# Strassen products over 12 instead of 8 of the 16 contraction chunks, with two of the three input sums sharing one refilled buffer

## The chip, the cores and the metric

The kernel runs on one core of a Trainium2 chip. The metric is the device time of one execution in microseconds (us). Times given as "of the profiled execution" come from one run that the hardware profiler recorded; its span runs from the first to the last instruction.

## What is computed

One inference step of a streaming encoder layer for 592 tokens (16 meta tokens, 512 prompt frames, 64 sample frames), in float32:

```python
z = jnp.einsum('bld,dc->blc', h, w_in)           # 592 x 2048 times 2048 x 6672
fq, fk, fv, fg, ff, sq, sk, sv, sg = jnp.split(z, idx, axis=-1)
fo = fox_prompt(fq, fk, fv, lf) * jax.nn.silu(fg)            # 16 forgetting heads
so = swa_prompt(sq, sk, sv, sinks, rel_bias) * jax.nn.silu(sg)  # 16 sliding-window heads
out = jnp.einsum('blc,cd->bld', jnp.concatenate([fo, so], axis=-1), w_out)
x = layer_norm(ALPHA * h + out, ln_g, ln_b)
```

`lf` is a log-sigmoid of `ff`, and its running sum enters the scores of the forgetting heads. Keys, values and `lf` are returned too.

## The kernel before, in words

A float32 product is made of three matmuls on a high and a low part of each operand (high by high, high by low, low by high); ScalarE writes the high part as a copy in a rounded format, VectorE the low part as a difference.

The projection has 52 tiles of 128 output columns. Tiles 0 and 1 are made in the opening (`opening_products`); the other 50 are taken two at a time, in 25 **duos** `d` = 1 to 25. The contraction is 2048 long, 16 **chunks** of 128. In a duo the 592 tokens are cut in two halves of 296 (`early`, `late`), the two tiles are the other direction, and over the first `2 * CUT` chunks Strassen's scheme is used: seven block products in place of eight, each over `CUT` chunks. Over the rest plain products are made. A duo is 15 **units** on TensorE (`unit`, u = 0 to 14): 0, 1, 2, 3, 6, 7 and 10 are block products of 3 x `CUT` matmuls; 4, 5, 8, 9, 11, 12, 13 and 14 are plain. Here `CUT` is 4, so that each of the 15 units has 12 matmuls. A matmul streams 296 columns, or 280 in the first half of a gate or query tile, where the meta tokens are not needed.

Three block products need sums of blocks of the input: `sum7` in unit 2, `sum6` in unit 1, `sum3` in unit 7. They are made once in the opening (`opening_splits`) and stay in SBUF, each as high and low part. The seven need sums of weights as well, which VectorE makes for every duo (`make_seven`, `make_five`, `make_six`, `make_four`), after which ScalarE and VectorE split them.

What a duo's weights go through: SyncE's queue loads the front part (`FRONT`, the first `2 * CUT` chunks) and the back part of tile f into `w_raw[f]`, in the order front 1 (after `right_low`), front 0 (after `four_made`), back 1, back 0 of the next duo. Splits and sums have fixed steps: `five_part` at u = 1 (ScalarE) and 2 (VectorE), `right_part` 2 and 4, back of tile 1 at 3 and 5, `four_part` 5 and 6, front of the next duo 7 and 8, `make_seven` and `make_five` 9, `make_six` 10, `seven_part` and `six_part` 11 and 12, back of tile 0 at 13 and 14. VectorE also takes TensorE's results out of PSUM (`take_six`, `take_seven`, `take_five`, and `join` at u = 6, 10, 13 and at the end, which sets `corner_summed`, `side_summed`, `top_summed`, `bottom_summed`). Unit 0 of the next duo waits for `top_summed`, unit 10 for `corner_summed` and `four_low`.

The attention of one pair of heads is woven into the same steps. A **stretch** is one or two duos with one pair: Fox stretches have two duos ("vg", the even one, with a value and a gate tile, then "qk"), and Swa stretches mostly one ("gq", a gate and a query tile: duos 18, 19, 20, 23, 24, 25). For each of five token tiles i, TensorE makes scores (`score`), VectorE adds terms and takes the maximum, ScalarE takes the exponential (`probabilities`) and scales the rows (`scale_rows`), TensorE turns them (`turn`), ScalarE copies what was turned (`keep_turned`), and TensorE multiplies by the values (`values`, which waits for `turned_read`). Scores are at steps 3, 6, 9, 12, 15 in stretches of two duos and at 1, 3, 5, 7, 9 in those of one, each turn is four steps later, and values(2) and values(3) of a gq duo are at step 13. Each engine works its own list in order.

The first stretch is duo 1 alone, without attention. After the opening VectorE and ScalarE make the input sums, and then the forget gates: `gate_inputs`, `gate_ones`, `gate_reciprocals` at s = 3, `gate_logs` at 5, `gate_sums` at 7. TensorE turns the sums after step `GATES_TURNED_AT` (9), VectorE copies them (`keep_gates`) at the end of step 10, and `turn_values`, at step `V_FIRST_AT` (13), waits for that copy (`cq_ready`). `bias_table`, some 30 small copies, is at VectorE's step 13.

After duo 25 the last pair's attention runs beside the first column tile of the output product, and then come the other three and the norm; the change leaves their code as it is, but for the order in which mixed rows are loaded.

## Time and profile before

| | us |
|---|---|
| median of 3 runs | 1024.56 (1023.91 to 1025.81) |
| the profiled execution | 1025.96 |
| its span | 1024.1 |
| opening, up to unit 0 of duo 1 | 42.2 |
| duo 1 | 30.9 |
| duos 2 to 25 | 727 |
| output product and norm | 224 |

A row of a timeline is start, duration, engine, line, operation, what it writes and reads, its shape and the count; a bracket gives the engine's idle time before it and what ended it. A matmul's duration runs longer than the distance to the next one, since they are pipelined: the distance of starts is what it costs.

### The profile page before, as it was taken

How to read it: one execution, taken by the hardware profiler on the slowest of the kernel's cores; microseconds unless marked ns; L12 is line 12 of the kernel's file. 1: busy time of each engine (PE TensorE's matmuls, PEld its weight loads, DVE VectorE, ACT ScalarE, POOL GpSimd, SP SyncE). 2: the span in 40 equal slices, each digit the busy share in tenths (PEclk: the TensorE clock that was granted, in tenths of full speed). 3: DMA queues.
4: the chain of work that ended last, by engine and by line, in shares of the span. 5: the costliest groups of instructions: out<-in, count | busy, mean ns of one | idle time of the engine just before them, and what ended most of it. 6: DMA issues, size and time to landing. Idle time of an engine off the chain costs nothing.

```text
span 1024.1 us, 20283 instructions
## 1 busy us (share of the span) xinstructions
PE 1002.4 (98%) x7287; PEld 940.2 (92%) x7287; DVE 717.8 (70%) x1454; ACT 531.6 (52%) x1217; POOL 66.7 (7%) x125
## 2 busy tenths in 40 slices
PE   8989999999999999999999999999999999999996
PEld 7889999999999999999999999999999888888884
DVE  5989676876868687686867787768787654141685
ACT  5537465564646555564565776656677652111400
POOL 1020100100010010001010000000000000000000
PEclk9999999999999999999999999999999999999998
DMA  8233433132343312333322322231226543222423
GB/s 329 72 100 109 140 110 127 58 109 97 109 139 109 125 54 102 107 109 128 120 75 69 102 81 93 102 105 51 88 81 233 189 171 103 83 82 82 165 68 117
DMA packets 36257, 115.05 MB, mean 112 GB/s; under 512 B 9312, under 2 KB 9728, under 8 KB 33584
## 3 DMA queue, kind: packets, MB, share of 16 engines
q1 hardware_dynamic: 24352, 87.26, 24.7%
q0 software_dynamic: 11856, 27.14, 7.9%
q8 instruction: 31, 0.51, 0.2%
q14 instruction: 18, 0.15, 0.0%
HBM read 99.31 MB, written 18.29 MB: 115 GB/s over the span
## 4 chain that ended last, share of the span: by engine, by line
PE 86%; DMA 5%; DVE 5%; issue 2%; ACT 2%; SPq 1%; DVEq 0%; ACTq 0%
PE ps L1627 28%; PE ps L1637 25%; PE ps L1874 20%; PE ps L1839 5%; PE ps L1813 4%; DMA w_raw<-in_w_all 3%; PE ps L1797 2%; PE ps L1796 2%; DMA x_raw<-in_xT 1%; DVE wl L1094 1%; PE ps L1859 1%; DVE tb L1271 1%; SPq L572 0%; ACT pt L939 0%; PE ps L1817 0%
## 5 line engine op out<-in xcount | busy, mean ns | idle before, releaser
L1627 PE MATMUL ps<-xh,wh 128*128 128x296 f32 (+1 forms) x864 | 261.4, 302 | 1.6 <-DVE wl L1357 1.5
L1627 PE MATMUL ps<-xh,wl 128*128 128x296 f32 (+1 forms) x864 | 257.4, 298 | 0.0
L1627 PE MATMUL ps<-xl,wh 128*128 128x296 f32 (+1 forms) x864 | 257.0, 297 | 0.0
L1874 PE MATMUL ps<-wh,mix_parts 128*128 128x512 f32 x576 | 185.2, 391 | 0.0
L1627 PEld LDWEIGHTS ps<-xh,wh 128*128 128x128 f32 x864 | 163.8, 190 | 5.8 <-issue 3.7
L1627 PEld LDWEIGHTS ps<-xl,wh 128*128 128x128 f32 x864 | 164.0, 190 | 0.0
L1627 PEld LDWEIGHTS ps<-xh,wl 128*128 128x128 f32 x864 | 163.4, 189 | 0.0
L1094 DVE TENSOR_TENSOR wl<-w_raw,wh 128x1024 fp32r<-128x1024 f32 (+1 forms) x150 | 142.9, 953 | 20.4 <-ACT wh L825 9.1
L1874 PEld LDWEIGHTS ps<-wh,mix_parts 128*128 128x128 f32 x576 | 108.1, 188 | 23.5 <-DVE rows L1562 0.4
L917 ACT ACTIVATE tb<-tb,small 128x256 f32<-128x256 f32 (+5 forms) x160 | 81.2, 508 | 92.1 <-DVE small L1290 64.2
L1874 PE MATMUL ps<-wl,mix_parts 128*128 128x512 f32 x320 | 124.9, 390 | 0.0
L1637 PE MATMUL ps<-xh,wh 128*128 128x296 f32 x400 | 121.4, 304 | 1.0 <-ACT vT L977 1.0
L1637 PE MATMUL ps<-xl,wh 128*128 128x296 f32 x400 | 119.3, 298 | 0.0
L1637 PE MATMUL ps<-xh,wl 128*128 128x296 f32 x400 | 119.1, 298 | 0.0
L1637 PE MATMUL ps<-sum_high,wh 128*128 128x296 f32 x300 | 92.0, 307 | 0.0
L1637 PE MATMUL ps<-sum_high,wl 128*128 128x296 f32 x300 | 89.7, 299 | 0.0
L1637 PE MATMUL ps<-sum_low,wh 128*128 128x296 f32 x300 | 89.6, 299 | 0.0
L1090 DVE TENSOR_TENSOR wl<-w_raw,wh 128x1024 fp32r<-128x1024 f32 x32 | 38.1, 1222 | 69.1 <-ACT wh L819 69.0
L929 ACT ACTIVATE tb<-tb,small 128x256 f32<-128x256 f32 (+4 forms) x160 | 71.7, 495 | 10.0 <-DVE small L1305 9.8
L1637 PEld LDWEIGHTS ps<-xh,wh 128*128 128x128 f32 x400 | 75.2, 188 | 1.3 <-ACT vT L977 1.2
L1637 PEld LDWEIGHTS ps<-xl,wh 128*128 128x128 f32 x400 | 75.4, 188 | 0.0
L1637 PEld LDWEIGHTS ps<-xh,wl 128*128 128x128 f32 x400 | 75.1, 188 | 0.0
(196 smaller groups left out, 1721.0 us busy)
## 6 DMA issues: line engine op xcount, KB each, us to landing
w_raw<-in_w_all SPq DMA_DIRECT2D x106, 512.0 KB, 4.4
w_raw<-in_w_all SPq DMA_DIRECT2D x14, 1024.0 KB, 4.8
cbc<-c_rows POOLq DMA_DIRECT2D x16, 360.0 KB, 4.1
x_raw<-in_xT SPq DMA_DIRECT2D x7, 592.0 KB, 9.6
rows<-in_x_p POOLq DMA_DIRECT2D x4, 1024.0 KB, 5.2
out_y_p<-rows SPq DMA_DIRECT2D x16, 256.0 KB, 2.6
mix_rows<-mixT POOLq DMA_DIRECT2D x14, 288.0 KB, 2.4
rel_copies<-rel_rows POOLq DMA_DIRECT2D x8, 384.0 KB, 10.7
```

The source lines that it names most:

```text
L917: nc.scalar.activation(t, t, ACT.Exp, bias=nm, accum_out=total[:, i % 3, head:head + 1]).then_inc(exp_done, 1)
L929: nc.scalar.activation(row, row, ACT.Copy, scale=recip[:, i % 3, head:head + 1]).then_inc(scaled, 1)
L1090: nc.vector.tensor_tensor(wl[slot][:, a], w_raw[slot % 2][:, a], wh[slot][:, a].bitcast(F32), ALU.subtract).then_inc(w_low, 1)
L1094: nc.vector.tensor_tensor(low, raw, high.bitcast(F32), ALU.subtract).then_inc(done, 1)
L1271: ins = nc.vector.scalar_tensor_tensor(out=rows_[:, head, a:b], in0=st.score_out(ps, head, piece, b - a), scalar=cqp[:, i, head:head + 1], ...
L1627: ins = nc.tensor.matmul(ps[:, bank, result(tile, h)], a[f][:, w], b[:, ko, first:first + width], start=(ko == n_first and i == 0), stop=( ...
L1637: ins = nc.tensor.matmul(ps[:, bank, 0:HALF], a[:, w], b[:, j, :], start=(start and j == 0 and i == 0), stop=(stop and j == CUT - 1 and i ...
L1796: nc.tensor.matmul(out, queries, k2[:, head, a:b], start=True, stop=False)
L1797: ins = nc.tensor.matmul(out, queries, k_low[:, head, a:b], start=False, stop=True)
L1813: ins = nc.tensor.transpose(st.turn_out(ps, head, j), tb[:, i % SLOTS, head, first:first + P], ident[:])
L1839: ins = nc.tensor.matmul(ps[head_rows(head), bank, at:at + q], v_nat[:, block_, HD * head:HD * head + HD], moving[:, head, 0:q], start=(j ...
L1874: ins = nc.tensor.matmul(ps[:, bank, :], a, b[slot][:, w], start=(ko == 0 and i == 0), stop=(ko == KO - 1 and i == len(products) - 1))
```

## The change

`CUT` becomes 6, so that block products have 18 matmuls, and the plain units cover `REST` = 2 chunks, 6 matmuls each. The order of units, the steps of the splits and of the attention stay.

`sum6` and `sum3` share one buffer, `sum_both` (high and low part, 1776 KB in all). Both are written to DRAM once (`sum_rows`), and each is loaded back in every duo: `sum3` after unit 1 for unit 7, `sum6` after unit 7 for unit 1 of the next duo. `sum3` is first kept in `x_raw` and split in duo 1 (`last_sum`: ScalarE at step 2, VectorE at step 3).

In the first stretch the parameters move: gates turned after step 11, `keep_gates` at the end of step 12, `turn_values` at 14, `gate_reciprocals` from 3 to 5. `bias_table` goes to GpSimd. SyncE's small loads go behind the loads of x, one weight load goes to ScalarE's queue. GpSimd waits for `sum_low` 4 earlier in its list. ScalarE copies the values before it splits the late block of x. The loads of front parts of duo 1 wait for both halves of the opening's weights.

```diff
-CUT = KO // 4
+CUT = 3 * KO // 8
+REST = (KO - 2 * CUT) // 2
-GATES_TURNED_AT, TABLE_AT, V_FIRST_AT = 9, 13, 13
+GATES_TURNED_AT, V_FIRST_AT = 11, 14
-MIX_PARTS = [(0, 2), (2, 5), (5, 8), (8, 12), (12, 14)]
+MIX_PARTS = [(0, 2), (2, 6), (6, 9), (9, 12), (12, 14)]
...
+        sum7_high, sum7_low = (sb(f"sum{n}", [P, CUT, HALF], F32R) for n in ("7_high", "7_low"))
+        sum_both = sb("sum_both", [P, 2, CUT, HALF], F32)
...
         def _(sp):
-            sp.dma_start(wff, w_ff).then_inc(wff_loaded, 16)
...
             for f in range(2):
-                sp.wait_ge(w_low, f + 1)
+                sp.wait_ge(w_low, f + 3)
                 load_part(1, f, FRONT, front_loaded)
             for f in range(2):
-                sp.wait_ge(w_low, f + 3)
                 load_part(1, f, BACK, back_loaded)
+            sp.wait_ge(sum_low, 2)
+            sp.dma_start(sum_rows[0], sum_both[:].rearrange("p a b c -> p (a b c)")).then_inc(sums_stored, 16)
             sp.wait_ge(back_low[0], 1)
             load_part(2, 0, BACK, back_loaded)
+            sp.wait_ge(sum_low, 4)
+            sp.dma_start(sum_rows[1], sum_both[:].rearrange("p a b c -> p (a b c)")).then_inc(sums_stored, 16)
+            sp.wait_ge(sums_stored, 32)
...
+            def load_sums(i, used, loaded):
+
+                sp.wait_ge(unit_done, used)
+                sp.dma_start(sum_both[:].rearrange("p a b c -> p (a b c)"), sum_rows[i]).then_inc(loaded, 16)
+
+            def load_three(d):
+
+                load_sums(1, UNITS * (d - 1) + 2, three_loaded)
+
+            def load_duo(d):
+
                 load_next_front(d, 1)
                 load_next_front(d, 0)
                 load_next_back(d)
+                load_sums(0, UNITS * (d - 1) + 8, six_loaded)
                 sp.wait_ge(back_low[0], d + 1)
                 load_part(d + 2, 0, BACK, back_loaded)
...
-                nc.vector.tensor_tensor(raw3[:], x12, raw6[:], ALU.subtract).then_inc(sum_made, 1)
+                dve.wait_ge(gates_summed, 1)
+                nc.vector.tensor_tensor(x11, x12, raw6[:], ALU.subtract).then_inc(sum_made, 1)
...
+            def last_sum():
+
+                dve.wait_ge(sum_high, 4)
+                low_of(both_low, x_raw[:, first_x, early], both_high, sum_low)
...
                 elif u in (4, 5):
                     if u == 4:
                         pe.wait_ge(back_low[0], d)
-                    ins = plain(0, 0, duo[0], TOP, range((u - 2) * CUT, (u - 1) * CUT), None)
+                    ins = plain(0, 0, duo[0], TOP, rest(u - 4), None)
...
                 elif u == 7:
+                    if st.first:
+                        pe.wait_ge(sum_low, 4)
+                    else:
+                        pe.wait_ge(three_loaded, 16 * d - 16)
```

## Rows read from the trace of the kernel before

**Rows 1.** Part 1 of the page: busy time of each engine.
```profile
PE 1002.4 (98%) x7287; PEld 940.2 (92%) x7287; DVE 717.8 (70%) x1454; ACT 531.6 (52%) x1217; POOL 66.7 (7%) x125
```

**Rows 2.** Windows: length, each engine's busy time (count), TensorE clock, DMA share, GB/s.
```profile
0.00:25.60 25.60, 22.39 (x138) 18.03 (x138) 15.35 (x16) 15.14 (x16) 2.77 (x14) 1.00 0.89 329
42.20:73.10 30.90, 27.45 (x192) 26.97 (x193) 26.87 (x64) 14.96 (x28) 5.67 (x12) 0.94 0.34 110
68.97:72.39 3.42, 3.42 (x16) 3.42 (x15) 2.86 (x13) 1.95 (x3) 0.00 (x0) 0.50 0.00 0
254.34:286.27 31.93, 31.93 (x263) 31.52 (x262) 25.63 (x53) 19.46 (x45) 2.19 (x3) 1.00 0.34 111
286.27:314.01 27.74, 27.74 (x223) 27.12 (x222) 18.76 (x40) 14.05 (x31) 2.69 (x5) 1.00 0.30 101
373.75:407.40 33.65, 32.33 (x263) 31.52 (x262) 25.63 (x53) 19.56 (x45) 2.19 (x3) 1.00 0.31 106
618.44:649.87 31.43, 31.43 (x262) 30.51 (x261) 24.80 (x57) 21.97 (x61) 1.77 (x3) 1.00 0.24 83
```

**Rows 3.** Chain that ended last, in order of time: start, us, what, count.
```profile
134.28 4.89 PE ps L1637 x36
...
384.15 7.59 DMA w_raw<-in_w_all
```

**Rows 4.** Groups by form: count, then busy us and mean ns of one.
```profile
L1094 DVE TENSOR_TENSOR wl<-w_raw,wh 128x1024 fp32r<-128x1024 f32 x75 | 91.5, 1220 | 17.1 <-ACT wh L825 9.1 <-ACT wh L831 7.9
L1094 DVE TENSOR_TENSOR wl<-w_raw,wh 128x512 fp32r<-128x512 f32 x75 | 51.4, 685 | 3.3
L831 ACT ACTIVATE wh<-w_raw 128x1024 fp32r<-128x1024 f32 x50 | 52.4, 1047 | 0.2
L837 ACT ACTIVATE wh<-w_sum 128x512 fp32r<-128x512 f32 x25 | 15.6, 626 | 2.2 <-DVE w_sum L1110 1.8
```

**Rows 5.** Timeline of duo 20 (gq), step 9 to values(2).
```profile
636.99 0.34 PE L1796 MATMUL ps<-k,q 128*128 128x192 f32 x1
...
638.41 0.29 PE L1627 MATMUL ps<-xl,wh 128*128 128x280 f32 x1
638.54 0.29 PE L1627 MATMUL ps<-xh,wl 128*128 128x280 f32 x1
...
639.13 0.69 DVE L1110 TENSOR_TENSOR w_sum<-w_raw 128x512 f32<-128x512 f32 x1
...
642.01 0.63 ACT L837 ACTIVATE wh<-w_sum 128x512 fp32r<-128x512 f32 x1
...
643.77 0.57 ACT L939 ACTIVATE pt<-ps 128x512 f32<-128x512 f32 x1
...
644.48 0.44 PE L1839 MATMUL ps<-pt,v_nat 128*64 128x128 f32 x4
```

**Rows 6.** Timeline of duo 8 (vg) before turn(1).
```profile
270.74 1.04 ACT L825 ACTIVATE wh<-w_raw 128x1024 fp32r<-128x1024 f32 x1
...
272.75 1.11 ACT L929 ACTIVATE tb<-tb,small 128x384 f32<-128x384 f32 x2
...
273.63 0.83 PE L1813 MATMUL ps<-ident,tb 128*128 128x128 f32 x6
```

**Rows 7.** Timeline, end of duo 7 (qk): the join behind `top_summed`, next unit 0.
```profile
251.47 0.46 DVE L1200 TENSOR_TENSOR mid_part<-ps,mid_part 128x296 f32<-128x296 f32 x1
...
254.34 0.30 PE L1637 MATMUL ps<-xh,wh 128*128 128x296 f32 x1
```

**Rows 8.** Timeline of the first stretch: TensorE's first unit, VectorE's copy, `turn_values`.
```profile
42.19 0.41 PE L1637 MATMUL ps<-xh,wh 128*128 128x296 f32 x1 [0.96 <-ACT vT L977]
...
67.33 0.15 DVE L1446 COPY cq<-ps 64x16 f32<-64x16 f32 x1
...
67.64 0.27 PE L1859 MATMUL ps<-ident,v_twice 128*32 128x128 f32 x1 [2.27 <-DVE cq L1446]
```

**Rows 9.** Part 6 of the page: DMA issues, KB each, median us to landing.
```profile
w_raw<-in_w_all SPq DMA_DIRECT2D x14, 1024.0 KB, 4.8
```

More of the change, by code:

```diff
@@ L572, in _ @@
                     sp.dma_start(x_raw[:, x_part(i), :], xT[:, x_part(i), :]).then_inc(x_loaded[i], 16)
-                else:
+                elif i != 1:
                     slot, a = w_part(i)
@@ L576, in _ @@
                 if what == "x" and i == 1:
+                    sp.dma_start(wff, w_ff).then_inc(wff_loaded, 16)
+                if what == "x" and i == X_PARTS - 1:
                     for dst, src in ((gate_half(bf, 0), b_f), (gate_half(bf, 1), b_f), (lfc, lf_cache), (relT, rel),
@@ L680, in _, with bias_table @@
             pool.wait_ge(own_made, 3)
+            def bias_table():
+                pool.wait_ge(small_loaded, 5 * 16)
+                for a, b, bucket in bias_runs():
+                    ins = nc.gpsimd.tensor_copy(bias_rows[:, a:b],
+                                                relT[:, bucket:bucket + 1].broadcast_to([16, b - a]))
+                ins.then_inc(bias_made, 1)
             def first_loads(st):
@@ L1016, in run @@
                             right_part(d, (unit_done, st.after(k, 1)))
+                        if st.first and u == 2:
+                            last_sum(st)
                         if u == 3:
@@ L1495, in run @@
                             five_part(d)
+                        if st.first and u == 3:
+                            last_sum()
                         if u == 4:
@@ L1642, in of_tile, with rest @@
                 return wh[f][:, part], wl[f][:, part]
+            def rest(i):
+                return range(2 * CUT + i * REST, 2 * CUT + (i + 1) * REST)
             def of_x(ko, columns):
@@ L1690, in unit @@
                         pe.wait_ge(back_low[1], d)
-                    ins = plain(1, 0, duo[1], SIDE, range((u - 6) * CUT, (u - 5) * CUT), None)
+                    ins = plain(1, 0, duo[1], SIDE, rest(u - 8), None)
                 elif u == 10:
@@ L1696, in unit @@
                 elif u in (11, 12):
-                    ins = plain(0, 1, duo[0], TOP, range((u - 9) * CUT, (u - 8) * CUT), None)
+                    ins = plain(0, 1, duo[0], TOP, rest(u - 11), None)
                 else:
@@ L1700, in unit @@
                         pe.wait_ge(under_made, d)
-                    ins = plain(1, 1, duo[1], BOTTOM, range((u - 11) * CUT, (u - 10) * CUT), 2 * CUT)
+                    ins = plain(1, 1, duo[1], BOTTOM, rest(u - 13), 2 * CUT)
                 ins.then_inc(unit_done, 1)
```

88 lines of the change are left out of this document (45 added, 43 removed).

## The prediction

> **What bounds the kernel now.** I read the page first: TensorE is busy for 1002.4 us, 98% of the span, with VectorE at 70% and ScalarE at 52% [rows 1]. A busy share alone doesn't say that shorter work on TensorE shortens the kernel, so I read windows next. A vg duo (duo 8), a qk duo and a gq duo have TensorE busy for their whole length, 31.93, 27.74 and 31.43 us [rows 2]: there is no idle time to recover, and every matmul taken away is worth its full pitch, as long as nothing else is just behind it. The same windows say who might be: in the vg and the gq duo VectorE is busy for 25.6 and 24.8 us and ScalarE for 19.5 and 22.0 us. The third reading is therefore the timeline at those places where TensorE takes over from ScalarE or VectorE: how long was the result there before it was used? That slack, not the busy share, decides this change.
>
> **Part 1, the matmuls.** 36 matmuls take 4.89 us, 0.136 us each [rows 3]; of 280 columns one takes 0.13 [rows 5]. Each duo gets 7 x 2 x 3 = 42 more in block products and 8 x 2 x 3 = 48 fewer in plain units. A vg or qk duo loses 36 wide and 12 narrow ones, 6.4 us, and gains 5.7: -0.73. A gq duo loses 24 and 24, 6.3 us: -0.65. With 19 and 6 of them that is 13.9 + 3.9 = -17.8 us.
>
> **Part 2, what VectorE and ScalarE get.** VectorE takes 1.22 us for 1024 elements and 0.685 for 512 [rows 4], so 0.15 + 1.045 per thousand: 0.95 for 768 and 1.75 for 1536. Per duo the front part costs 0.53 more, two back parts 1.07 less, five splits and four sums 9 x 0.27 = 2.4 more: +1.87. ScalarE, by its rows 0.21 + 0.82 per thousand, gets 0.42 - 0.84 + 5 x 0.21 = +0.6. Both have room by the share, 47 us on VectorE's 718. But the work is not spread evenly, and neither is what TensorE loses: steps with a block product get 0.81 us longer, plain ones 0.8 shorter. From unit 7 to unit 0 of the next duo there are six plain units and two block products, so the time is 3.2 us shorter there, just where seven, five, six and the front part are made.
>
> **Part 3, gq duos.** The chain in duo 20 [rows 5]: scores at 636.99, VectorE's `make_seven` at 639.13, `make_five`, the join, ScalarE's copies of q, seven high at 642.01, six high, scaling, `keep_turned` at 643.77 to 644.34, `values` at 644.48. The last row has no idle time ahead of it, so TensorE came there by itself, and the result was there 0.14 before: the slack is about 0.1. After the change, seven and five are 0.27 longer each, ahead of the join, and seven and six high 0.21 each: the chain takes 0.96 longer. TensorE goes through units 9, 11 and 12 at 0.8 less each and unit 10 at 0.8 more: it is there 1.6 us sooner. Stall: 0.96 + 1.6 - 0.1 = 2.4, I take 2.35. It stands in duos 18, 19, 20, 23 and 24: 11.8 us. In 18 and 23 VectorE enters late from the qk duo (below) and the front part reaches ScalarE late, +1 each (bounds 0 and 2). Duo 25 has no seven and six, but the 1.6 us; its slack is larger, +0.7. Sum: +14.5, bounds 8 and 20.
>
> **Part 4, vg duos.** In duo 8 ScalarE's front copy is at 270.74, the first scaled rows of tile 1 are ready at about 273.35, and TensorE turns them at 273.63 [rows 6]: slack 0.3. From scores(0) to this turn TensorE will need 0.7 less (plain units outweigh). VectorE's list in between (right, four +0.54, back -0.54, a wait of 0.4 for the exponential absorbed) is 0.45 shorter, ScalarE's front copy is 0.43 longer: stall 0.45 as the low end. What adds to it is the load of front 0. It is issued after `four_made`, at about 13.3 us in the duo. It is now 768 KB, behind 768 KB for tile 1 and behind `sum3`. For 1776 KB no row exists: 1024 KB take 4.8 us [rows 9] and the opening moves 329 GB/s [rows 2], so 4.8 + 0.77 MB / 0.329 = 7.1 us; bounds 4.8 and 8.3 (in proportion). `sum3` is issued at 5 and lands at 12, four before unit 7 needs it. Front 0 then lands at 18.3 to 20, against 18.4 when ScalarE is free: up to 1.6 more stall. The trace shows such a wait already: a front load of 7.59 us is on the chain [rows 3], and that duo takes 33.65 us against 31.93 [rows 2]; a third of that difference, 0.6, I take as the mean of the eight vg duos, already paid. I take a stall of 1.3 here and 0.2 at the next turn (the effect of part 3, with more slack), less 0.6 already there: +0.9 for each of 8, +7.2, bounds -2 and +14.
>
> **Part 5, qk duos.** The join behind `top_summed` ends at 251.93, unit 0 starts at 254.34: slack 2.4 [rows 7]. TensorE needs 2.1 us less from unit 9 to there, and the chain of six, seven low, six low and ScalarE's seven is 0.8 longer: stall 0.5 in nine qk duos (3 to 17, 22), and 0.3 in duo 21: +4.8, bounds 0 and 8.
>
> **Part 6, the first stretch.** TensorE now waits 2.27 us for VectorE's gate copy, done at 67.5 [rows 8], so VectorE's list sets this time, and all that is put ahead of the copy counts in full. Four sums of x and four low parts grow from 1184 to 1776 elements: 8 x 0.62 = 4.95. The weight work of duo 1 and of the next front, sums included: +3.2. `keep_gates` goes behind seven low and six low: 1.9. The loads of duo 2's front parts are behind the store of `sum3` on SyncE's queue, with a wait for it: `sum3` is split in step 3, at about 56, stored by 63, fronts land at 67 to 69, while VectorE is through with `gate_sums` by 68: it waits some 3 us for ScalarE's front copy. Against that the x loads start about 2 us earlier, for the small loads are behind them: -1.5. The copy is done at 67.5 + 11.5 = 79. `bias_table` on GpSimd takes 2.2 us off VectorE, but behind this wait. TensorE then goes through one unit, not two: duo 2 starts 9.5 us later than now. Before that the wait for `vT` [rows 8] stays about as it is. Beside the -0.73 already counted this is +10.2, bounds 4 and 13.
>
> **One rule beside a row.** After the 2.27 us wait the clock was at 0.50, the lower of its two levels, 1.2 GHz, for 3.42 us [rows 2], and units 13 and 14 cost 0.8 us more each. The Trainium skill (TensorE: Matmul & The Clock Gate, "What's actually happening") says that the throttled state is the default and activity releases it; by that rule, which the trace supports here, new stalls can cost more than their own length. That is a rival below.
>
> **The sum.** -17.8 + 14.5 + 7.2 + 4.8 + 10.2 = +18.9 us. Store and loads of the sums, mixed rows in other portions and the output stage cost nothing by themselves: the loads have four to eight us of slack, and the portions have the last units of duo 25 ahead of them; without that cover the first output step would wait 2 or 3 us. The profiled execution took 1025.96, span 1024.1 plus 1.9 around it, and is 1.4 above the median; the difference goes on the median: 1024.56 + 18.9 = 1043.5, say 1043.
>
> **Rivals.**
> (a) The clock falls in the gq duos too. The wait there is as long as the one after which it fell, and small matmuls follow. At 1.7 us for each of six: 1053. For: the one row. Against: duo 12's stall of 1.5 us left the clock at 1.00.
> (b) Transfers bind. If the big loads get 220 GB/s beside the others (two thirds of the opening's 329), front 0 lands 2 us later again: +2 in eight vg duos, +1.6 in six gq duos, +26: 1069. Against: the DMA share is 0.24 to 0.34 now and gets to about 0.5.
> (c) Faster: slack is larger than I read. If `keep_turned` and `top_summed` stay ahead of TensorE, because the joins start earlier with the shorter units, parts 3 and 5 vanish and part 4 is at its low end: -17.8 - 2 + 10 = 1015. It turns to faster when the stalls of parts 3 to 6 stay below 17.8 together. Against: the slack of 0.1 in rows 5 is read directly.
> (d) The change balances out: low ends of parts 3 and 6, the rest at nothing: within 0.2%.
>
> **Numbers.** Forecast 1043 (1033 to 1051): 0.54. (a) 0.18, (b) 0.11, (c) 0.12, (d) 0.05. Faster 0.13, same 0.05, slower 0.82, where 0.2% (2 us) is about what a measurement can tell from no change. The range leaves out (b)'s upper part and most of (c): 1024 to 1062.
>
> **What would show it.** In the new profile: idle before `values` (ScalarE's `pt` copy as releaser) of some 2.3 us in each gq duo; idle before turn(1) in vg duos, with front loads on the chain; unit 0 behind VectorE's join in vg duos; duo 2 starting near 82 us; no wait on the sums. VectorE busy near 770 us. If gq duos last under 31 us, part 3 is wrong, and if duo 2 starts before 76 us, part 6.

## The result and the profile after

The changed kernel takes 1138.51 us (median, 1132.37 to 1142.33), the kernel before 1025.12 beside it (1023.91 to 1025.81). The ratio is 1.1104, 95% interval 1.1065 to 1.1142. The forecast was 1043, the range 1024 to 1062: the sign was right, the size off by 95 us. The profiled execution took 1138.23, its span is 1136.7 against 1024.1.

The page after: busy time of each engine (as in [rows 1]), the chain that ended last by engine, and the two largest kinds of transfer (KB each, median us from issue to landing).

```profile
PE 1017.3 (89%) x7137; PEld 948.2 (83%) x7137; DVE 764.5 (67%) x1423; ACT 552.2 (49%) x1217; POOL 83.4 (7%) x156
...
PE 52%; DMA 17%; DVE 13%; issue 9%; ACT 8%; DVEq 0%; SPq 0%; ACTq 0%
...
sum_both<-sum_rows SPq DMA_DIRECT2D x48, 1776.0 KB, 7.7
w_raw<-in_w_all SPq DMA_DIRECT2D x52, 768.0 KB, 7.0
```

TensorE's busy time rose by 15 us although it has fewer matmuls, and its share fell from 98% to 89%. The first goes with a lower clock (0.963 over the span, 0.995 before), the second is waiting. So the next view is the list of TensorE's waits: first of the kernel before, then of the changed one. Columns: who waits for whom, us in total, times, longest.

```profile
PE ps L1813 <- ACT tb L929: 3.2, 4, 1.3
PE ps L1859 <- DVE cq L1446: 2.3, 1, 2.3
```
```profile
PE ps L1860 <- ACT tb L963: 41.0, 10, 5.9
PE ps L1676 <- DVE mid_part L1243: 22.7, 9, 4.4
PE ps L1906 <- DVE mixT L1362: 11.2, 7, 2.6
PE ps L1906 <- DVE cq L1486: 11.1, 1, 11.1
PE ps L1886 <- ACT pt L973: 10.9, 7, 1.8
PE ps L1886 <- ACT pt_meta L975: 3.2, 5, 0.9
```

Each line is one place of the schedule: the turns of the vg duos (`tb`), unit 0 behind the join (`mid_part`), `turn_values` of the qk duos (`mixT`) and of the first stretch (`cq`), `values` of the gq duos (`pt`, `pt_meta`). 100 us stand there, and before 5.5 at the first and the fourth place and nothing at the others. All of these places but the third were in the prediction; the first is several times what it said.

Windows of the changed kernel, for [rows 2]: the opening, duo 1, the low clock behind its wait, duo 8 (vg), duo 9 (qk), duo 12 (vg), duo 20 (gq).

```profile
0.00:25.60 25.60, 22.05 (x127) 17.36 (x128) 16.64 (x17) 15.46 (x16) 2.79 (x14) 1.00 0.93 349
45.10:86.34 41.24, 28.13 (x186) 27.40 (x186) 32.98 (x50) 18.33 (x30) 11.45 (x33) 0.83 0.47 171
75.66:89.31 13.65, 5.69 (x25) 5.68 (x26) 10.29 (x24) 7.59 (x17) 2.84 (x7) 0.50 0.28 85
292.49:331.78 39.29, 34.30 (x256) 33.65 (x256) 28.06 (x55) 21.89 (x48) 2.19 (x3) 0.91 0.47 164
331.78:362.41 30.63, 27.28 (x218) 26.24 (x216) 19.90 (x37) 13.29 (x29) 2.71 (x5) 1.00 0.67 235
433.04:473.13 40.09, 34.73 (x255) 34.08 (x256) 27.98 (x55) 21.78 (x48) 2.19 (x3) 0.87 0.44 161
714.91:748.38 33.47, 31.31 (x256) 29.83 (x254) 26.49 (x57) 22.68 (x61) 1.77 (x3) 1.00 0.52 186
```

The vg duo takes 39.29 against 31.93, the qk duo 30.63 against 27.74, the gq duo 33.47 against 31.43; of those shown only the qk and the gq duo keep the clock at 1.00. Summed over the trace, from the start of one duo to the next, the 112.6 us of span stand in: the time up to duo 2 +13.3, the eight vg duos 2 to 16 +50.8, the eight qk duos 3 to 17 +25.7, the six gq duos +18.3, duos 21 and 22 +6.1, the output stage -1.4.

Why a vg duo is 7 us longer is seen in duo 8, in the chain that ended last (start, us, what) and in the timeline beside it, for [rows 6]:

```profile
305.97 9.60 DMA w_raw<-in_w_all
```
```profile
315.67 1.48 ACT L859 ACTIVATE wh<-w_raw 128x1536 fp32r<-128x1536 f32 x1 [4.66 <-DMA w_raw<-in_w_all]
...
318.12 1.10 ACT L963 ACTIVATE tb<-tb,small 128x384 f32<-128x384 f32 x2
...
318.77 1.54 PE L1860 MATMUL ps<-ident,tb 128*128 128x128 f32 x6 [4.99 <-ACT tb L963]
```

Front 0, 768 KB, is 9.6 us on its way and lands at 315.57, 23.1 us into the duo. ScalarE has been idle for 4.66 us by then, and TensorE waits 4.99 at turn(1). The prediction had it land at 18.3 to 20. It isn't the refill ahead of it that is in the way: the 1776 KB for `sum3` were issued at 297.68 and landed 7.4 us later, before front 0 was issued. What else is under way from 297 on is a copy of 384 KB, `rel_copies<-rel_rows`, on GpSimd's queue: issued at 297.01, it lands 17.9 us later. The list of transfers of the kernel before, then of the changed one:

```profile
rel_copies<-rel_rows POOLq DMA_DIRECT2D x8, 384.0 KB, 10.7
```
```profile
rel_copies<-rel_rows POOLq DMA_DIRECT2D x8, 384.0 KB, 18.3
```

### The profile page after: what moved, and what is told of

Its sections match the earlier page's. It is cut to its first block, busy times and chain, and to the rows that moved or that the text cites. A ratio compares the mean times of both kernels' runs of the same rounds, so it can differ in the third digit from the quotient of the medians.

```text
span 1136.7 us, 20065 instructions
## 1 busy us (share of the span) xinstructions
PE 1017.3 (89%) x7137; PEld 948.2 (83%) x7137; DVE 764.5 (67%) x1423; ACT 552.2 (49%) x1217; POOL 83.4 (7%) x156
## 4 chain that ended last, share of the span: by engine, by line
PE 52%; DMA 17%; DVE 13%; issue 9%; ACT 8%; DVEq 0%; SPq 0%; ACTq 0%
PE ps L1676 21%; PE ps L1921 18%; DMA w_raw<-in_w_all 16%; PE ps L1666 6%; DVE wl L1137 3%; PE ps L1886 2%; PE ps L1860 2%; DVE w_sum L1171 2%; ACT wh L859 2%; ACT pt L973 1%; DVE w_sum L1153 1%; DVE tb L1314 1%; PE ps L1844 1%; ACT tb L963 1%; PE ps L1843 1%
## 5 line engine op out<-in xcount | busy, mean ns | idle before, releaser
L1676 PE MATMUL ps<-xh,wh 128*128 128x296 f32 x600 | 191.9, 320 | 27.0 <-DVE mid_part L1243 22.7
L1137 DVE TENSOR_TENSOR wl<-w_raw,wh 128x1536 fp32r<-128x1536 f32 (+1 forms) x150 | 149.7, 998 | 81.9 <-ACT wh L859 77.0
L1676 PE MATMUL ps<-xh,wl 128*128 128x296 f32 x600 | 188.0, 313 | 0.0
L1676 PE MATMUL ps<-xl,wh 128*128 128x296 f32 x600 | 187.6, 313 | 0.0
L1676 PEld LDWEIGHTS ps<-xh,wh 128*128 128x128 f32 x600 | 122.1, 204 | 30.0 <-DVE mid_part L1243 16.9
L1666 PE MATMUL ps<-xh,wh 128*128 128x296 f32 (+1 forms) x464 | 143.4, 309 | 1.9 <-DMA pt<-in_w_ff 1.9
L1666 PE MATMUL ps<-xl,wh 128*128 128x296 f32 (+1 forms) x464 | 138.6, 299 | 0.0
L1666 PE MATMUL ps<-xh,wl 128*128 128x296 f32 (+1 forms) x464 | 138.4, 298 | 0.0
L1676 PE MATMUL ps<-sum_both,wh 128*128 128x296 f32 x600 | 126.3, 303 | 0.0
L1676 PEld LDWEIGHTS ps<-sum_both,wh 128*128 128x128 f32 x600 | 97.0, 189 | 0.8
L1676 PE MATMUL ps<-sum_both,wl 128*128 128x296 f32 x300 | 89.7, 299 | 0.0
## 6 DMA issues: line engine op xcount, KB each, us to landing
x_raw<-in_xT SPq DMA_DIRECT2D x7, 592.0 KB, 11.9
```

What stands on the lines that cost most here:

```text
L1137: nc.vector.tensor_tensor(low, raw, high.bitcast(F32), ALU.subtract).then_inc(done, 1)
L1666: ins = nc.tensor.matmul(ps[:, bank, result(tile, h)], a[f][:, w], b[:, ko, first:first + width], start=(ko == n_first and i == 0), stop=( ...
L1676: ins = nc.tensor.matmul(ps[:, bank, 0:HALF], a[:, w], b[:, j, :], start=(start and j == 0 and i == 0), stop=(stop and j == CUT - 1 and i ...
```

## Experiments

Theory T1: the front loads land late beside the refills, perhaps because of that copy (T1a), perhaps by the traffic alone (T1b). Rival T2: the larger pieces on VectorE and ScalarE are what costs. Most kernels below have one execution. The changed kernel's own four lie within 10 us of each other, so differences under 5 us between two of its variants are not read, and those from 5 to 10 with caution. A stall is given as the trace's bracket has it. The expectations count most of them from the distance of starts, which adds 0.13 to 0.2 us: their 1.93 us ahead of `values`(3) is a bracket of 1.79, their 2.30 one of 2.17.

### The refills left out

```diff
-                load_sums(1, UNITS * (d - 1) + 2, three_loaded)
-                load_sums(0, UNITS * (d - 1) + 8, six_loaded)
-                        pe.wait_ge(six_loaded, 16 * d - 16)
-                        pe.wait_ge(three_loaded, 16 * d - 16)
```

> The changed kernel without the refills: from duo 2 on sum_both is never loaded again and TensorE's two waits on the loads are gone, so every unit 1 after duo 1 multiplies by sum3 in place of sum6 (this part of the computation is left out). Theory T1 (the front loads land late beside the refills, and with them ScalarE's and VectorE's front copies, turn(1) in vg duos and unit 0 after qk duos): vg duos fall from 38.9 us to about 32.5, qk duos from 30.9 to about 28.3, so 1138 - 8 x 6.4 - 9 x 2.6 = about 1064, bounds 1055 to 1075. Rival T2 (the larger splits and sums on VectorE and ScalarE beside shorter plain units, parts 3 to 5 of the prediction, make the loss; the transfers are hidden): the stalls stay, over 1125. In both the 1.9 us ahead of values(3) in gq duos stay, and duo 2 still starts near 86.

Measured: 1075.68. TensorE's waits:

```profile
PE ps L1675 <- DVE mid_part L1242: 17.6, 9, 2.2
PE ps L1856 <- ACT tb L962: 12.8, 10, 2.0
PE ps L1902 <- DVE cq L1485: 11.5, 1, 11.5
PE ps L1882 <- ACT pt L972: 10.7, 6, 1.8
```

63 us go with the refills: the turns fall from 41.0 to 12.8, and `turn_values` behind `mixT` from 11.2 to 0.6. But 51 us over the kernel before stay, and the waits at unit 0 and at `values` stay as well: T1 holds for one part, T2 has another.

### SyncE's wait for the stores moved

```diff
-            sp.wait_ge(sums_stored, 32)
...
                 load_next_back(d)
+                if isinstance(d, int):
+                    sp.wait_ge(sums_stored, 32)
                 load_sums(0, UNITS * (d - 1) + 8, six_loaded)
```

> The changed kernel with SyncE's wait for both stores of the sums moved from ahead of duo 2's front loads to ahead of the first refill. The front loads then go out right behind the second store is issued, at about 59 in place of 64.8 (if four_made and right_low of duo 1 are there by then). If the late front parts hold up the first stretch: duo 2 starts 3 to 5 us earlier than 86.3, 1134 or so. Rival: VectorE's list ahead of the gate copy is what sets turn_values, the fronts wait for four_made or share the engines with the store: within 1 us, 1137 to 1139.

Measured: 1141.51, duo 1 lasts 40.63 in place of 41.24. The front loads go out at 58.78 in place of 64.83, beside the store then, and VectorE's wait ahead of `front_low` shrinks from 2.95 to 2.35 us only. Duo 2 starts at 84.67 in place of 86.34: less than the 3 to 5 us of the theory, and not clear of the noise, since kernels below that change nothing in the first stretch start it at 83.5 to 86.4. SyncE's wait is at most a small part of what holds up the first stretch.

### The copies moved, and the size of the cut

All eight `rel_copies` copies at the end of the first stretch:

```diff
                 pool.wait_ge(bias_stored, 16)
+                for i in range(BIAS_COPIES):
+                    copy_bias(i)
...
-                if st.kind is Fox:
-                    copy_bias(st.g)
```

> The changed kernel with the 384 KB copies rel_copies<-rel_rows, one at the start of each of eight stretches, issued all eight in a row at the end of the first stretch (nothing is left out). Theory T1a (these copies, landing in 17.9 us beside the refill of sum3, slow the refill and the two front loads): in duos 8 to 16 the front loads land 2 to 4 us earlier and these five vg duos last 35 to 37 us in place of 39.3 to 40.1, against some loss in duos 2 to 5: 1138 - 15, bounds 1112 to 1130. Rival T1b (the refills' own 3.5 MB per duo are the load, the copy is a bystander): duos 8 to 16 as before within 0.5 us, 1135 to 1142.

Measured: 1103.37, below the bounds given. Duo 2, beside all eight copies, is 40.49 long; the vg duos from 4 on last 33.0 to 34.9 (39 to 40 in the changed kernel, duo 6 38.3). The copies are no bystander: 35 us go with them, with every refill in place. Then the old cut, with refills and the changed first stretch (the rest of the edit only places the smaller buffers):

```diff
-CUT = 3 * KO // 8
+CUT = KO // 4
...
```

> The changed kernel with Strassen's products over 8 of the 16 chunks, as the kernel before has them: shared buffer, refills (1184 KB in place of 1776), order of the first stretch and of the mixed rows stay as changed. T1 (refills): two thirds of the transfer per duo is left, so front 0 (512 KB behind 512 KB and 1184 KB) lands some 3 us after where it did before; vg duos 34 to 36 us, qk duos 28 to 30: 1025 + 8 x 3 + 9 x 1 + 8 for the first stretch = 1066, bounds 1045 to 1085. T2 (larger pieces on VectorE and ScalarE): their sizes are the old ones here, so all but the first stretch is as before: 1025 to 1035.

Measured: 1062.12. Windows of duos 8, 9 and 20:

```profile
268.83:305.90 37.07, 33.75 (x264) 33.06 (x262) 25.73 (x53) 19.62 (x45) 2.19 (x3) 0.95 0.50 161
305.90:333.64 27.74, 27.74 (x224) 27.11 (x222) 18.79 (x40) 14.05 (x31) 2.70 (x5) 1.00 0.53 189
655.54:686.97 31.43, 31.43 (x261) 30.51 (x260) 24.83 (x57) 21.97 (x61) 1.76 (x3) 1.00 0.45 158
```

The two theories part by duo: duos 9 and 20 are to the hundredth those of [rows 2], so there is no loss there without the wider cut and its larger loads; the vg duo is 5 us longer with the old sizes, so 5 of its 7 us need only the transfers. Duo 2 starts at 78.34 (73.09 before): 5.3 of the 13.3 us of the first stretch are there at the old sizes, with its new order and the stores (6.5 in the next kernel). Now both, the old cut and each copy held until the refill of `sum6` has landed:

```diff
-                if st.kind is Fox:
-                    copy_bias(st.g)
...
+                if st.kind is Fox:
+                    pool.wait_ge(six_loaded, 16 * st.duo(0))
+                    copy_bias(st.g)
```

> The changed kernel with products over 8 of the 16 chunks (as in e_cut4: 1184 KB refills, changed first stretch) and each rel_copies copy held until the refill of sum6 has landed. If the stall needs both refill and copy (T1a), vg duos come back to some 32 us and only the first stretch (duo 2 starts at 78.3 in place of 73.1) is left: 1025 + 5 = 1030, bounds 1026 to 1033. If refills alone cost (T1b): 1045 to 1062, vg duos at 34 to 37.

Measured: 1026.39. Duo 8:

```profile
259.13:291.06 31.93, 31.93 (x263) 31.53 (x262) 25.64 (x53) 19.46 (x45) 2.19 (x3) 1.00 0.52 182
```

2.4 MB more per duo (DMA share 0.52 in place of 0.34) and not a hundredth of a microsecond lost. T1b falls for this size: refills alone cost nothing in duos 3 to 25, refills beside the copy 36 us. And the kernel before, its copies held until unit 7 of the vg duo:

```diff
+                if st.kind is Fox:
+                    pool.wait_ge(unit_done, st.after(0, 7))
+                    copy_bias(st.g)
```

> The kernel before, with each of its eight rel_copies copies held on GpSimd's queue until unit 7 of the vg duo is done (some 18 us into the duo, when no weight load is under way) in place of the duo's start; nothing else is changed, nothing left out. Theory T1a (the copy slows the front loads that are under way beside it, in the kernel before as well: the 7.59 us load on its chain): the stalls ahead of turn(1) in duos 2, 4, 12 and 14 (1.16, 0.37, 1.48, 0.79 us) and what follows them go, vg duos last 31.8 to 32.0 throughout: about 1020, bounds 1018 to 1022. Rival T1b (the long front load has another cause): 1024 to 1025.

Measured: 1021.38 (1020.89 to 1021.68), ratio 0.9965, interval 0.9953 to 0.9977. The vg duos 4 to 16 last 31.94 to 32.03 each, and the load of [rows 3] takes 4.27 us in place of 7.59. So its length, which the prediction took as a trait of the load, was this copy's doing.

### The wide cut without refills, and with small pieces

The changed kernel with the edit that leaves out the refills and the one that holds back the copies (here until unit 8 is done):

> The changed kernel without refills (as in a_no_refill; every unit 1 after duo 1 multiplies by sum3, which leaves out that part) and with the copies held until unit 8 of the vg duo: what is left is the wider product itself with the larger pieces on VectorE and ScalarE, and the first stretch. If refill and copy only hurt together: like a_no_refill less its small turn(1) stalls (1.1 to 2.1 us, to about 0.5): 1076 - 9 = 1067, bounds 1060 to 1072. If the copy alone costs nothing: 1074 to 1077. If the larger pieces were cheap, as the forecast had it for qk duos (stall at unit 0 of 0.5 us in place of the 2.1 seen): under 1055.

Measured: 1081.21, outside all three bounds and by 5 us worse than with the copies at their old time, the clock being 0.974 against 0.979: without refills the copy costs nothing that can be read. What is left are four waits, on the first stretch and on VectorE and ScalarE:

```profile
PE ps L1676 <- DVE mid_part L1243: 17.7, 9, 2.2
PE ps L1857 <- ACT tb L963: 11.9, 10, 1.5
PE ps L1903 <- DVE cq L1486: 11.3, 1, 11.3
PE ps L1883 <- ACT pt L973: 10.8, 6, 1.8
```

The same with the pieces of VectorE and ScalarE at their old sizes from duo 2 on (the helper is put into every sum and split):

```diff
+        def old(d, part):
+            if isinstance(d, int) and d == 1:
+                return part
+            return slice(part.start, part.start + (part.stop - part.start) * 2 // 3)
...
-                low_of(wl[1][:, A], w_raw[0][:, A], wh[1][:, A], six_low)
+                low_of(wl[1][:, old(d, A)], w_raw[0][:, old(d, A)], wh[1][:, old(d, A)], six_low)
```

> As m_neither (no refills, later copies, wide products on TensorE) but from duo 2 on VectorE's and ScalarE's pieces have the sizes of the kernel before: sums and splits 512 columns in place of 768, front parts 1024 in place of 1536; the back parts stay at 512. The last third of each piece is not computed; that part is left out, beside that of m_neither. TensorE's work is the same. T2 (the larger pieces are what costs, 1081 in m_neither): stalls at unit 0 of qk to vg (2.1 to 2.4 us) and at turn(1) (1.0 to 1.7) go, gq keeps 1.4 of its 1.93, since TensorE is still 1.6 sooner there; about 1025, bounds 1015 to 1038. Rival T4 (the shorter plain units, TensorE arriving sooner, and transfers of 768 KB make the stalls whatever the pieces' size): over 1060.

Measured: 1028.06. Waits, and windows of duos 9 and 20:

```profile
PE ps L1908 <- DVE cq L1491: 7.4, 1, 7.4
PE ps L1888 <- ACT pt L978: 5.9, 6, 1.7
PE ps L1862 <- ACT tb L968: 3.0, 8, 0.6
```
```profile
292.65:319.73 27.08, 27.08 (x217) 26.27 (x215) 17.13 (x37) 11.80 (x29) 2.71 (x5) 1.00 0.37 127
620.47:652.36 31.89, 31.06 (x255) 29.89 (x254) 23.62 (x57) 21.46 (x61) 1.76 (x3) 1.00 0.24 81
```

53 us go with a third of the columns: T2 is right for what refill and copy leave over. The qk duo now shows the gain that was hoped for, 27.74 - 27.08 = 0.66 us with TensorE busy throughout. The vg duos don't: those without a stall above 0.35 us last 32.0 to 32.1, against 31.93. The gq duo keeps 0.83 us ahead of `values`(3) (expected 1.4, counted from starts) and is 0.46 longer than before: the shorter plain units alone cost the gq duo more than they give.

A cut in between, 10 of 16 chunks, copies held back, nothing left out:

> The changed kernel with products over 10 of the 16 chunks (refills of 1480 KB, pieces of 640 in place of 768 or 512, plain units of three chunks) and each rel_copies copy held until the refill of sum6 has landed. Nothing left out. Measured ends: 8 chunks with later copies 1026.4, 12 chunks with later copies 1103.8. If each stall is a slack overrun, as parts 3 to 5 of the prediction work it out, half the growth gives less than half the loss, since the first part only eats slack: qk duos keep their 27.4 (slack 2.4), gq duos wait about 1.1 us (0.48 + 0.8 - 0.1) and last 32.2, vg duos 31.9: 1026 - 4 + 5 + 4 for the first stretch = 1031, bounds 1024 to 1042. If the loss is in proportion to the size: 1065.

Measured: 1047.60, outside both. Duos 8, 9 and 20 last 32.90, 28.14 and 32.70; 18 and 23, not foreseen, 35.4 and 37.1. The loss starts within the first step of size and bends upward, 21 us for the first 2 chunks, 50 to 56 for the next (from here to the kernels at 12 chunks whose copy does no harm, 1097.89 to 1103.80).

### Which refill, and the order in the gq duos

The refill of `sum3` alone left out, copies held back:

```diff
-                load_sums(1, UNITS * (d - 1) + 2, three_loaded)
...
-                        pe.wait_ge(three_loaded, 16 * d - 16)
```

> The changed kernel with later copies and only the refill of sum3 (the one released after unit 1, ahead of the two front loads on SyncE's queue) left out; the refill of sum6 stays, and every unit 7 after duo 1 multiplies by sum6 (that part is left out). With both refills and later copies: 1101 to 1104, qk duos 30.4 to 31.9 with 1.3 to 2.6 us ahead of turn_values. With neither: 1081, qk duos 29.0 to 29.6 without that stall. If it is the refill of sum3 that pushes the front loads of qk duos back: qk duos 29.0 to 29.6, stall under 0.5: about 1083, bounds 1078 to 1089. If it is the traffic of both as such: 1090 to 1100.

Measured: 1079.70, qk duos 28.4 to 29.6, no wait behind `mixT`. With both refills that wait is 8.8 to 12.5 us in total. It is the refill of `sum3`, issued just ahead of the front loads on the same queue, that makes them late in the qk duos; the refill of `sum6` costs nothing that can be read (1081.21 with neither).

For the gq duos first VectorE's reciprocals and ScalarE's scaling were put ahead of the two high parts:

```diff
+                        if u == 11 and len(st.duos) == 1 and not st.first:
+                            scale_rows(st, 4)
                         if u == 11 and not last:
                             seven_part(d + 1, (unit_done, st.after(k, 10)))
```

> The changed kernel with two edits that act in different duos, nothing left out: the rel_copies copies held until the refill of sum6 has landed (vg duos), and in gq duos VectorE's reciprocals of the last piece ahead of the join at unit 10, ScalarE's scaling of that piece ahead of the high parts of seven and six. T1a: vg duos 33.2 as in c_copies_early, duo 2 included (35 in place of 40.5). Part 3 of the prediction (the chain of five larger pieces ahead of the scaling makes the stall ahead of values(3)): the 1.93 us fall to 0.5 or less and gq duos from 33.5 to 34.4 to about 32.5, the clock dips behind them going too. Sum 1103 - 5 - 7 = 1091, bounds 1085 to 1096. Rival to part 3 (another chain, VectorE's scores or the q splits, is just as late): the stall stays over 1.4 and gq duos over 33.2.

Measured: 1103.80. The stall grew from 1.79 to 2.17 us and three of the four duos 19, 20, 24 and 25 with it: refuted. It is `keep_turned`(3), behind both high parts, that TensorE waits for. So that one was put ahead:

```diff
+                        if u == 11 and st.kind is Swa and len(st.duos) == 1:
+                            keep_turned(st, 3)
```

> The changed kernel with the copies held until the refill of sum6 has landed and, in gq duos, ScalarE's copy of turned piece 3 (pt) put ahead of the high parts of seven and six (in k_copies_later_gq only the scaling was put ahead, the copy stayed behind it, and the stall grew to 2.30). Nothing left out. If the stall ahead of values(3) is this copy behind the two high parts (2 x 0.83 us) and behind VectorE's larger seven and five: it falls from 1.93 to 0.3 or less, and gq duos 19, 20, 24, 25 last 32 us or less in place of 33.9 to 35.3: 1104 - 6 x 2.2 = about 1090, bounds 1086 to 1096. If the stall then stands ahead of the next values instead, or the clock stays down for another reason: over 1099.

Measured: 1101.12, as the second condition has it. The 1.79 us ahead of `values`(3) are gone, and 1.16 ahead of turn(4) and 1.24 ahead of the last `values` are there in their place. With both edits:

> The changed kernel with later copies and both edits of ScalarE's order in gq duos together: the copy of turned piece 3 (pt) and then the scaling of piece 4 ahead of the high parts of seven and six (VectorE's reciprocals of piece 4 one step earlier with it). Nothing left out. Alone, the scaling ahead left 2.30 us ahead of values(3), and the copy ahead turned the 1.93 us there into 1.29 ahead of turn(4) and 1.40 ahead of the last values. If it is ScalarE's order, with the two larger high parts ahead of both, all three stalls fall to 0.4 or less and gq duos 20, 24 and 25 last 31.5 to 32.2 in place of 34.2 to 36.4: about 1101 - 12 = 1089, bounds 1084 to 1094. If VectorE's list is just as late: a stall over 0.8 stays at one of the three places, over 1095.

Measured: 1116.35, the worst of the three. Timeline of ScalarE in duo 20:

```profile
710.61 0.60 ACT L974 ACTIVATE pt<-ps 128x512 f32<-128x512 f32 x1
711.24 0.80 ACT L964 ACTIVATE tb<-tb,small 128x192 f32<-128x192 f32 x2
711.94 0.83 ACT L872 ACTIVATE wh<-w_sum 128x768 fp32r<-128x768 f32 x1
712.68 0.83 ACT L878 ACTIVATE wh<-w_raw 128x768 fp32r<-128x768 f32 x1
715.23 0.45 ACT L918 ACTIVATE first_part<-mid_part 128x296 f32<-128x296 f32 x1 [1.73 <-DVE mid_part L1250]
...
716.11 0.58 ACT L974 ACTIVATE pt<-ps 128x512 f32<-128x512 f32 x1
```

TensorE gets pieces 3 and 4 in time, but seven's high part now starts at 711.94. VectorE's two low parts (712.80 and 713.87) and then the join (`mid_part`, 714.74) are behind it, and ScalarE's next copy of `pt` is behind the join: TensorE waits 3.38 us for it. ScalarE and VectorE hand work to each other in a ring here. The larger pieces are in the ring, and an edit of the order on one engine moves the stall along it.

### What is wrong with the copy

Held back, with no other transfer under way, the copy still took 10.2 us for 384 KB, where 512 KB of weights take 3.9. This is one such copy in the kernel before with its copies held back, in the columns of [rows 2]: the DMA engines are busy for 0.15 of the time, which is the work of two to three of the 16, and move 46 GB/s.

```profile
391.00:399.50 8.50, 8.50 (x87) 8.24 (x85) 7.88 (x20) 6.57 (x18) 0.09 (x1) 1.00 0.15 46
```

From the second copy on, the source was made the copies of the first two heads, in the changed kernel and in the kernel before:

```diff
+                pool.dma_start(rel_copies[two], rel_copies[0:2]).then_inc(bias_copied, 16)
```

> The changed kernel with its refills and with the eight 384 KB copies at their old place and time, but from the second on the source is the first two heads' copies (384 KB in a piece) in place of two rows of 1536 bytes read 128 times each; the bias of the other heads is left out that way. If the shape of the copy (two short rows read over and over) slows the loads beside it: landing in some 5 us in place of 17.9, vg duos at 33 to 34 from duo 6 on, 1138 - 30 = about 1107. If any memory to memory copy of GpSimd's queue beside the refill does it, or its 0.4 MB as such: 1130 to 1142.

> The kernel before with its copies at their old place and time, but from the second on from the first two heads' copies (384 KB in a piece) in place of two rows read 128 times each; the bias of the other heads is left out that way. If the shape of the copy is what slows the front loads, in the kernel before as well: as g_before_copies_later, 1021, vg duos at 31.9 to 32.0. If the place in time is what counts: 1024 to 1025 with stalls ahead of turn(1) in three or four vg duos.

Measured: 1097.89, the copies from the new source landing in 3.6 us; and 1021.80 for the kernel before (4.4 us). This changed the source and the way in which the copy is cut. So the cut alone:

```diff
-                pool.dma_start(rel_copies[two], rel_rows[two, :].rearrange("h (o n) -> h o n", o=1)
-                               .broadcast_to([2, P, REL])).then_inc(bias_copied, 16)
+                pool.dma_start(rel_copies[two].rearrange("h p n -> p h n"),
+                               rel_rows[two, :].rearrange("h (o n) -> o h n", o=1)
+                               .broadcast_to([P, 2, REL])).then_inc(bias_copied, 16)
```

> The changed kernel, refills and copies at their old times, with one edit: the rel_copies copy is written with the 128 rows as its outermost dimension (128 x 2 x 384) in place of the two heads (2 x 128 x 384). Same bytes from the same two rows read 128 times each, nothing left out. The plain copy of r_plain_copy changed two things at once, the source and the way the copy is cut over the engines. If the outermost dimension of two confines the copy to few of the 16 DMA engines, and the big loads wait for these (the Trainium skill, DMA: Bandwidth & Descriptors, Rules for kernel authors, says that an outermost dimension below 16 does that): the copy lands in some 4 to 6 us in place of 18.3 and the time is that of r_plain_copy, 1098, bounds 1092 to 1106. If reading two short rows over and over is what is slow, whatever the cut: 1130 to 1142.

> The kernel before with the same single edit (the 128 rows outermost in the rel_copies copy), copies at their old place and time, nothing left out. If the cut over the engines is the cause: as v_before_plain, 1021 to 1022, a ratio of 0.997 to the kernel before. If the two rows read over and over are: 1024 to 1025, ratio 1.000.

Measured: 1098.05 for the changed kernel, and 1021.33 for the kernel before (1020.92 to 1022.11), ratio 0.9962, interval 0.9948 to 0.9975. The list of transfers of the changed kernel with this edit:

```profile
rel_copies<-rel_rows POOLq DMA_DIRECT2D x8, 384.0 KB, 4.9
```

4.9 us in place of 18.3, for the same bytes from the same two rows. Reading short rows over and over costs the kernel nothing that can be read (the copy lands in 4.9 us, from the contiguous source in 3.6); the outermost dimension of two was the fault. In duo 8 front 0 is now under way for 5.5 us, against 9.60. The Trainium skill (DMA: Bandwidth & Descriptors, Rules for kernel authors) says that an outermost dimension below 16 confines a DMA to at most that many of the 16 engines. The runs agree with it (10.2 us alone in the one form at a DMA share of 0.15, 4.9 to 5.1 beside other loads in the other); which engines carried it no view here shows.

Of the 4.4 us that the kernel before gains in span by this edit, 3.6 stand in duos 4 to 16; 0.8 are there at the start of duo 3 already.

## Why the prediction was wrong, step by step

The kernels above split the 112.6 us of span. Wide cut and first stretch without refills: 55.6 (m_neither's span 1079.7). The refills, with a copy that does no harm: 16.9 more (w_spread, 1096.6), mostly `sum3`'s ahead of the qk duos' fronts. The badly cut copy beside the refills: 40.1 more. By place, in us against the kernel before (single executions; the forecast's column has each part with its share of the -17.8):

| | forecast | changed | copy well cut (w_spread) | no refills (m_neither) |
|---|---|---|---|---|
| up to duo 2 | +9.5 | +13.3 | +12.3 | +13.3 |
| eight vg duos | +1.4 | +50.8 | +10.6 | +11.9 |
| qk duos, with 21 and 22 | -2.5 | +31.8 | +31.1 | +14.4 |
| six gq duos | +10.6 | +18.3 | +19.8 | +16.7 |
| output stage | 0 | -1.4 | -1.4 | -0.8 |
| span | +18.9 | +112.6 | +72.5 | +55.6 |

Of the 94 us that the forecast lacks, 49 are in the vg duos and 34 in the qk duos. So two steps failed, part 4 and part 5. Without the bad copy the kernel would still be at 1098, outside the range.

**What bounds the kernel, part 1, part 2: right, but for the vg duos.** The term of -0.73 for a qk duo measures -0.66 where nothing stalls. In the vg duos of the same kernel (small pieces) it doesn't show: 32.0 to 32.1 us with stalls up to 0.35, against 31.93. VectorE is at 764.5 us, 770 was said.

**Part 3, gq duos: the mechanism right, the place right.** 1.79 us ahead of `values`(3) behind ScalarE's `pt` (1.93 counted from starts), for 2.35. Duos 19, 20, 24 and 25 became 1.7 to 2.5 longer (2.35 - 0.65 = 1.7 forecast). Mis-sized are 18 and 23, 4.4 and 5.3 longer: the late entry from the qk duo was priced at 1 us, and unit 0 alone stalls 3.1 and 4.4 there. All gq duos together +18.3, for the forecast's 14.5 - 3.9 = 10.6.

**Part 4, vg duos: the step that failed by most.** It took a third of duo 12's excess as a trait of the load, "already paid", and let front 0 land at 18.3 to 20. The trace showed an instance that was 3 us slower than its median and I didn't ask what else was under way: the copy. Beside a refill the same copy lasts 18.3 us in place of 10.7, and front 0 lands at 23.1. With it: turns 41.0 us, vg duos +50.8 for a forecast of 7.2 - 5.8 = +1.4. Without it (w_spread): turns 12.4 us in ten stalls, near the 1.3 forecast for each. The eight vg duos then take 271.2 us against 260.6, +10.6. The forecast of +1.4 lacks the clock: a vg duo of w_spread that keeps it lasts 32.8 to 33.3 us. Six of them begin behind a stall of 2.16 to 2.17 us at unit 0; four of these have a mean of 0.95 and last 34.3 to 34.9, two keep 1.00. Duos 4 and 6, with the same 2.16:

```profile
149.73:184.59 34.86, 33.39 (x255) 32.44 (x256) 27.42 (x54) 21.61 (x48) 1.25 (x2) 0.95 0.54 186
216.37:249.53 33.16, 31.87 (x255) 30.92 (x256) 27.55 (x54) 21.51 (x48) 1.25 (x2) 1.00 0.55 194
```

**Part 5, qk duos: this failed too, by a time too small and by a wait that is missing.** The stall of 0.5 was 2.1 us less on TensorE plus 0.8 more on VectorE, less 2.4 of slack. Here VectorE's rows, first of the kernel before (duo 9), then of the kernel without refills (duo 9): the low front part and the join.

```profile
301.04 1.21 DVE L1094 TENSOR_TENSOR wl<-w_raw,wh 128x1024 fp32r<-128x1024 f32 x1
...
311.15 0.46 DVE L1200 TENSOR_TENSOR mid_part<-ps,mid_part 128x296 f32<-128x296 f32 x1
```
```profile
325.20 1.76 DVE L1136 TENSOR_TENSOR wl<-w_raw,wh 128x1536 fp32r<-128x1536 f32 x1 [1.05 <-ACT wh L858]
...
336.05 0.46 DVE L1242 TENSOR_TENSOR mid_part<-ps,mid_part 128x296 f32<-128x296 f32 x1
...
336.56 0.40 PE L1675 MATMUL ps<-xh,wh 128*128 128x296 f32 x1 [2.18 <-DVE mid_part L1242]
```

In both, the front part starts 0.9 us ahead of unit 8. From unit 8 to the end of unit 14 TensorE took 12.07 us (301.94 to 314.01) and now takes 8.1 (326.13 to 334.2): 4.0 less, not 2.1. From the front part's start to the join's end VectorE took 10.57 and now takes 11.31: 0.7 more. 4.0 + 0.7 - 2.4 = 2.3, what stands there (a bracket of 2.18). I had begun to count at unit 9 and from a later piece. Even from unit 9 the prediction's own 0.8 per unit gives 3.2 (five plain units shorter, one block product longer), so the 2.1 was also summed wrongly. This accounts for most of the 17 us between +14.4 and -2.5 in the table. The wait behind `mixT`, 11.2 us, was not in the prediction at all: `gate_heads`, which makes `mixT`, comes behind `front_low` on VectorE, and the front loads of the qk duo stand behind a 7 us refill on SyncE's queue. The prediction looked at that queue for vg duos only. The refills cost the qk duos another 17 us (31.1 against 14.4).

**Part 6, first stretch: right in kind, bounds just missed.** Duo 2 starts 13.3 us later; 9.5 was said, with bounds of 4 to 13 for the 10.2 that belong to it. The waits named are there: the one for `vT`, 2.32 us where it should have stayed at the 0.96 of [rows 8], and one long one for `cq`. One of 1.9 us for VectorE's `wl`, 21.5 us into duo 1, was not named:

```profile
45.10 0.61 PE L1676 MATMUL ps<-xh,wh 128*128 128x296 f32 x1 [2.32 <-ACT vT L1009]
...
73.09 1.76 DVE L1137 TENSOR_TENSOR wl<-w_raw,wh 128x1536 fp32r<-128x1536 f32 x1 [2.95 <-ACT wh L859]
...
83.32 0.16 DVE L1486 COPY cq<-ps 64x16 f32<-64x16 f32 x1
```

The 3 us that VectorE was to wait for the front part are there (2.95), the copy is at 83.3 where 79 was said. Duo 1 starts 2.9 us late, where the forecast gave the opening 1.5 back. Behind the wait the clock is at 0.50 for 13.65 us (first windows above), for 3.42 in [rows 2].

**The sums.** No wait on `six_loaded` or `three_loaded` in any list: as said. The output stage is 1.4 shorter (222.0 against 223.4 us): next to nothing, as said.

**The rivals.** (a), the clock in gq duos: the 1.79 us left it at 1.00 in duos 19, 20 and 24, so (a) is wrong there; in duos 18 and 23, behind the longer stalls at unit 0, it is at 0.95 and 0.93. In m_neither, with a stall of 1.80, gq duo 20 has 0.95 and lasts 34.35. It fell in the vg duos, where no rival had put it (0.91 and 0.87 in the windows above). (b) was the right sign-post: transfers bind, front 0 lands late. But its price was 2 us per vg duo, from a rate shared among the loads, and that traffic alone costs nothing at the old cut; it had a chance of 0.11 and gave 1069. (c) and (d) needed slack that isn't there.

The range was too narrow for three reasons. No interval had a second transfer on the same engines whose length depends on the first (40 us). The stall at unit 0 was counted over too short a stretch, and the qk duos' front loads were not followed behind the refill (34 us together). And the forecast priced stalls of 2 us without the clock that can fall behind them.

## What to carry to other kernels

Before transfers are added, list all others that are under way at that time and look at each one's KB per microsecond against its neighbours: one at a third of the usual rate (384 KB in 10.7 us beside 512 in 4.4) is worth a question by itself, and the loads beside it paid more here when traffic grew. One rearranged dimension is worth 4 us in the kernel before (1021.33 against 1025.26) and 40 in the changed one (1098.05 against 1138.51).

When work is moved between block products and plain units, take the stretch between a split's start and the join that it delays, and count both engines over that same stretch. Where two engines hand work to each other in a ring, a change of order on one can move the stall and not remove it: three changes of order did so here, and only smaller pieces made it shorter.

## What the runs showed of the hardware

A copy with an outermost dimension of two kept the DMA engines at a share of 0.15 when nothing else was under way (10.2 us for 384 KB), and slowed large loads beside it: the 768 KB load of front 0 in duo 8 took 9.60 us beside it, and 5.5 once the copy was cut over 128 rows. At the old cut, with the copies held back, 2.4 MB of refills per duo cost nothing beside 2 MB of weights at a DMA share of 0.52.

The clock fell to 0.50 after some stalls of a given length and not after others: in w_spread, of six stalls of 2.16 to 2.17 us ahead of a vg duo, four were followed by a duo with a mean of 0.95 and two by one at 1.00. The changed kernel's four executions lie 10 us apart, where the kernel before varies by 2 to 3. That the clock makes this difference is likely (0.963, 0.963, 0.956 and 0.953 in the four), but not shown: the two at 0.963 differ by 6 us themselves.
